# Two heads' attention scores in the row halves of TensorE's array, with the gate sums added by VectorE

## The chip, the cores and the metric

The kernel runs on one core of one Trainium2 chip. The metric is the device time of one execution in microseconds. The engines are TensorE (PE in the profile, its weight loads PEld), VectorE (DVE), ScalarE (ACT), GpSimd (POOL) and SyncE (SP), which here only issues transfers.

## What is computed

Four post-norm layers over 256 positions of width 1024. Layers 0 and 3 mix tokens by forgetting attention ("fox": 16 heads of 64, causal, with a bias from cumulated log forget gates), layer 1 by an S5 state-space mixer, layer 2 by pooling. Each mixer is followed by a norm, a SwiGLU FFN and a norm. What matters here:

```python
log_f = jax.nn.log_sigmoid((x @ w_f + b_f))
c = jnp.cumsum(log_f, axis=1)                       # per position and head
logits = einsum('bqhd,bkhd->bhqk', qb, k) * scale   # scale = 1/8
logits = logits + cb[..., :, None] - c_k[..., None, :]
logits = jnp.where(mask, logits, -inf)              # causal
p = softmax(logits)                                 # then p @ v, @ w_o
```

The term of the query, cb, is the same along a row and drops out of the softmax; the kernel adds only the key's term, kept as eight times the negated sum, so that the scale of the exponential (0.125) serves both.

## The kernel before

Weights stream as tiles of 128 x 1024 f32 (512 KB). SyncE loads a tile into one of four raw buffers once VectorE is done with the tile four earlier; ScalarE rounds it to a high half (L617, semaphore w_hi), VectorE subtracts for the low half (L1021, w_lo), and TensorE forms three products of every pair of operands in place of one (L1628 to L1630, 256 columns; L1637 to L1643, 512 columns). `w_used` counts the tiles that TensorE is done with, and frees their places. Each engine's order is the order in which the code for that engine is written; engines meet only in semaphores.

A fox layer has tiles 0 to 7 for V, then for each of eight pairs of heads p one tile for Q and one for K, then tiles 24 to 31 for the output projection. The loop step j of TensorE does the products of Q and K of pair j (banks 4 and 5), turns the probabilities of pair j-2 (L1931, `probs_turned`), forms the scores of pair j-1 (L1948 and L1949) and the output products of pair j-2 (L1960, L1961; head s writes to PSUM partitions 64s to 64s+63, so each head has a half of the array's columns). Pair 7's scores and the last two pairs' probabilities follow among the first output projections (`out_half`).

Queries and keys are copied head by head from PSUM to buffers of 80 partitions (L783 by ScalarE, L1283 by VectorE): 64 of the head, and 16 rows below in which the keys' buffer holds the gate sums of all heads (L754) and the queries' buffer a one for the head's own row (L747 in layer 0 by ScalarE, L566 in layer 3 by GpSimd). The score product so adds the gate sums itself. VectorE then adds the causal mask and takes the row maxima (L1255 for the first 128 queries, L1257 for the others, `masked`), ScalarE takes the exponentials (L800, L802), VectorE scales (`scaled`, L1244 to L1246).

GpSimd computes parameters of the S5 layer in `s5_parameters` (L486 to L532) during the first attention: a flag `zz_ready` (L525) lets VectorE scale the B matrices (`s5_scale`, L1372, from j = 5 on). Then it fills a piece of slot[2] with zeros and stores it eight times to `toep` in HBM (L573), and loads the rows of the norm (L584). The matrices B and C of the S5 layer come through SyncE's queue (L453) into slot[1] and slot[3]; ScalarE changes C's signs at L812 and L816, at the end of the fox layer.

Behind the last output projection VectorE forms the residual sum and statistics of the norm (L1037, L1041, `ln`); TensorE turns the normed activations next (L1608).

## Time and profile before

| | |
|---|---|
| median of 3 runs | 1169.89 us (1168.87 to 1171.18) |
| the profiled execution | 1169.65 us |
| its span, first to last instruction | 1167.9 us |
| busy: TensorE, weight loads, VectorE, ScalarE, GpSimd | 1150.9, 1068.3, 819.2, 601.4, 161.3 us |
| mean granted clock of TensorE | 0.999 of full speed |
| moved by DMA | 221.14 MB, mean 189 GB/s |

The span leaves out what lies around the instructions, so the time is 1.75 us above it. Matmuls are pipelined: the start of one to the start of the next tells how long it holds TensorE, its own duration is longer. A row "x6" is several instructions merged, with the time from the first's start to the last's end. In rows of a window, the busy times of the engines stand in order, each with its number of instructions.

### The profile page before, as it was taken

To read this page: it belongs to the slowest core of one execution; us is meant where nothing else is said; L and a number is where in the kernel's file an instruction comes from. 1 tells how busy PE (TensorE), PEld (TensorE's weight loads), DVE (VectorE), ACT (ScalarE), POOL (GpSimd) and SP (SyncE) were. 2 spreads that over 40 slices of the span, in tenths; PEclk is the share of its full clock that TensorE was granted. 3 is DMA by queue.
4 is the path that set the end of the run, shared out by engine and by line. 5 is a ranking of instruction groups with operands and counts; after the bars stand their busy time and mean duration, and the time that the engine had idled before them with its cause. 6 is when DMAs were issued, how large, how long until landed. Compare 5 with 4: busy or idle time off the path is not lost.

```text
span 1167.9 us, 22245 instructions
## 1 busy us (share of the span) xinstructions
PE 1150.9 (99%) x9166; PEld 1068.3 (91%) x9166; DVE 819.2 (70%) x1263; ACT 601.4 (51%) x947; POOL 161.3 (14%) x212
## 2 busy tenths in 40 slices
PE   8999999999999999999999999999999999999997
PEld 7998899999977779999998899999989988999996
DVE  7789899989868687455466776554587768654545
ACT  6777544544445456354444555444438664644441
POOL 0650099002970000000000000000010000000000
PEclk9999999999999999999999999999999999999999
DMA  6676454554756558565654556656536334856540
GB/s 243 219 269 228 160 198 151 193 181 175 235 167 211 181 180 300 178 226 180 202 170 162 198 180 236 201 180 205 190 101 241 130 109 146 277 188 200 182 163 37
DMA packets 63981, 221.14 MB, mean 189 GB/s; under 512 B 8068, under 2 KB 9988, under 8 KB 63368
## 3 DMA queue, kind: packets, MB, share of 16 engines
q1 hardware_dynamic: 57224, 202.57, 50.8%
q0 software_dynamic: 5648, 15.73, 4.1%
q8 instruction: 73, 1.20, 0.4%
q10 hardware_dynamic: 1008, 1.41, 0.4%
q14 instruction: 28, 0.23, 0.1%
HBM read 211.03 MB, written 7.60 MB: 187 GB/s over the span
## 4 chain that ended last, share of the span: by engine, by line
PE 93%; DVE 4%; DMA 1%; ACT 1%; issue 1%; SPq 0%; DVEq 0%; ACTq 0%
PE bank L1660 18%; PE bank L1628 15%; PE bank L1629 15%; PE bank L1630 15%; PE bank L1758 5%; PE bank L1692 4%; PE bank L1637 3%; PE bank L1643 3%; PE bank L1639 3%; DMA raw<-in_w 1%; PE bank L1949 1%; PE bank L1608 1%; PE bank L1793 1%; PE bank L1931 1%; PE bank L1960 1%; PE bank L1948 1%
## 5 line engine op out<-in xcount | busy, mean ns | idle before, releaser
L1021 DVE TENSOR_TENSOR wlo<-raw,whi 128x1024 fp32r<-128x1024 f32 x227 | 288.3, 1277 | 61.2 <-ACT whi L617 60.3
L617 ACT ACTIVATE whi<-raw 128x1024 fp32r<-128x1024 f32 x227 | 239.0, 1056 | 76.5 <-PE bank L1660 29.1
L1628 PE MATMUL bank<-xboth,whi 128*128 128x256 f32 x936 | 261.3, 279 | 0.0
L1629 PE MATMUL bank<-xboth,whi 128*128 128x256 f32 x936 | 259.3, 277 | 0.0
L1630 PE MATMUL bank<-xboth,wlo 128*128 128x256 f32 x936 | 259.2, 277 | 0.0
L1021 DVE TENSOR_TENSOR ext<-raw,ext 128x1024 fp32r<-128x1024 f32 x142 | 172.3, 1222 | 42.3 <-ACT ext L617 42.1
L1628 PEld LDWEIGHTS bank<-xboth,whi 128*128 128x128 f32 x936 | 176.2, 188 | 1.1 <-issue 0.9
L1629 PEld LDWEIGHTS bank<-xboth,whi 128*128 128x128 f32 x936 | 175.9, 188 | 0.1
L1630 PEld LDWEIGHTS bank<-xboth,wlo 128*128 128x128 f32 x936 | 175.8, 188 | 0.0
L617 ACT ACTIVATE ext<-raw 128x1024 fp32r<-128x1024 f32 x142 | 148.9, 1056 | 45.8 <-PE bank L1660 22.5
L1628 PE MATMUL bank<-xboth,ext 128*128 128x256 f32 x600 | 167.2, 279 | 0.0
L1629 PE MATMUL bank<-xboth,ext 128*128 128x256 f32 x600 | 166.0, 277 | 0.0
L1630 PE MATMUL bank<-xboth,ext 128*128 128x256 f32 x600 | 166.0, 277 | 0.0
L1169 DVE TENSOR_TENSOR hval<-bank,silu 128x256 f32<-128x256 f32 x80 | 33.8, 423 | 159.8 <-PE bank L1630 159.7
L1628 PEld LDWEIGHTS bank<-xboth,ext 128*128 128x128 f32 x600 | 112.8, 188 | 0.9 <-issue 0.9
L1629 PEld LDWEIGHTS bank<-xboth,ext 128*128 128x128 f32 x600 | 112.8, 188 | 0.1
L1630 PEld LDWEIGHTS bank<-xboth,ext 128*128 128x128 f32 x600 | 112.7, 188 | 0.0
L703 ACT ACTIVATE hhi<-hval 128x256 fp32r<-128x256 f32 x72 | 30.0, 417 | 127.5 <-DVE hval L1169 125.4
L698 ACT ACTIVATE silu<-bank 128x256 f32<-128x256 f32 x80 | 30.5, 381 | 99.3 <-PE bank L1630 99.3
L584 POOL DMA_DIRECT2D slot<-in_ln_row x16 | 8.6, 545 | 446.0 <-DVE x_tm L1093 395.7
L1660 PE MATMUL bank<-ext,hhi 128*128 128x256 f32 x448 | 61.8, 281 | 0.0
L1660 PE MATMUL bank<-whi,hlo 128*128 128x256 f32 x376 | 59.6, 281 | 0.0
(383 smaller groups left out, 2036.1 us busy)
## 6 DMA issues: line engine op xcount, KB each, us to landing
raw<-in_w SPq DMA_DIRECT2D x370, 512.0 KB, 4.3
slot<-in_ln_row POOLq DMA_DIRECT2D x16, 512.0 KB, 5.1
toep<-slot POOLq DMA_DIRECT2D x8, 512.0 KB, 8.5
toepA<-toep SPq DMA_DIRECT2D x2, 1024.0 KB, 6.5
BT<-toep SPq DMA_DIRECT2D x2, 1024.0 KB, 7.3
x_tm<-in_x SPq DMA_DIRECT2D x2, 512.0 KB, 5.2
slot<-in_s_B SPq DMA_DIRECT2D x2, 512.0 KB, 5.6
slot<-in_s_C SPq DMA_DIRECT2D x2, 512.0 KB, 5.8
```

Of the source, the lines that this page charges most:

```text
L617: nc.scalar.activation(hi_of(c), raw[:, c % RAW, :], ACT.Copy).then_inc(w_hi, 1)
L1021: V.tensor_tensor(lo_of(c), raw[:, c % RAW, :], hi_of(c).bitcast(F32), ALU.subtract).then_inc(w_lo, 1)
L1169: V.tensor_tensor(hval[:, :], bank[5][:, 0:SEQ], silu[:, :], ALU.mult).then_inc(h_ready, 1)
L1628: mm(dst, wh, bhi[:, kc, :], start=(i == 0), stop=False)
L1629: mm(dst, wh, blo[:, kc, :], start=False, stop=False)
L1630: ins = mm(dst, wl, bhi[:, kc, :], start=False, stop=(i == len(chunks) - 1))
L1637: mm(banks[2 * m + j][:, :], a_hi[:, cols], hi_of(c)[:, j * HALF:(j + 1) * HALF], start=first, stop=False)
L1639: mm(banks[2 * m + j][:, :], a_hi[:, cols], lo_of(c)[:, j * HALF:(j + 1) * HALF], start=False, stop=False)
L1643: ins = mm(banks[2 * m + j][:, :], a_lo[:, cols], hi_of(c)[:, j * HALF:(j + 1) * HALF], start=False, stop=last)
L1660: ins = mm(banks[2 * m + q // 2][:, q % 2 * SEQ:(q % 2 + 1) * SEQ], a[:, cols], w[:, q * SEQ:(q + 1) * SEQ], start=start and q % 2 == 0, s ...
L1692: return mm(banks[b][:, :], (a_lo if lo_act else a_hi)[:, cols], (lo_of if lo_w else hi_of)(c)[:, half], start=False, stop=stop)
L1758: return mm(out, x[:, kc, m * P:(m + 1) * P], w[:, 0:4, kc * P:(kc + 1) * P], start=start, stop=stop)
```

## The change

- **Scores.** Queries and keys of a pair lie in 128 partitions, head 0 in 0 to 63 and head 1 in 64 to 127, one copy for both. The scores of a head are a product over 64 rows of the array; the order is now both heads' 128-column products, then both heads' 256-column products.
- **Gate sums.** VectorE adds a tile `decay` in place of the constant mask: gate sums of the keys, the same in all partitions, with the mask in it. GpSimd makes it: it stores the gate sums to HBM (`gates_out`), loads them spread to 128 partitions pair by pair (`decay_load`, 256 KB), and adds the mask (`decay_causal`, two additions of 256 columns a pair). `masked` waits for it. In layer 0 eight such stops are put ahead of and into `s5_parameters`; in layer 3 they are a loop by itself, in which each load waits for a query copy.
- **Zeros.** The stores of zeros start before the gate sums, and go on one a stop.
- **C.** C's loads move behind the attention (its buffer slot[3] now holds masked sums), ahead of the weight tiles F0 + 2 = 34 and F0 + 3 = 35; its sign changes move to chunks 3 and 4 of the first FFN.
- The rows of ones and the copies of gate sums below keys and queries go.

```diff
@@ SyncE
+                if c in (F0 + 2, F0 + 3):
+                    part = slice((c - F0 - 2) * D, (c - F0 - 1) * D)
+                    sp.wait_ge(s_sb, HEADS)
+                    sp.dma_start(slot[3][:, part], t["s5_C"][:, part]).then_inc(c_landed, 16)
@@ GpSimd
+            def gates_out(f):
+                pool.wait_ge(gate_c, f + 1)
+                pool.dma_start(gates, zg[:, 0, :]).then_inc(gates_stored, 16)
+                pool.wait_ge(gates_stored, 16 * (f + 1))
+            def decay_load(f, p):
+                heads = slice(2 * p, 2 * p + 2)
+                pool.dma_start(decay_of(f)[:, heads, :, :].rearrange("p h j k -> p (h j k)"),
+                               gates[heads, :].rearrange("h k -> (h k)").partition_broadcast(P)).then_inc(decay_landed[p % 2], 16)
+            def decay_causal(f, p):
+                decay, corner = decay_of(f), corner_of(f)
+                tri = cst[:, C_MASK:C_MASK + P].unsqueeze(1).to_broadcast([P, 2, P])
+                heads = slice(2 * p, 2 * p + 2)
+                pool.wait_ge(decay_landed[p % 2], 16 * (PAIRS // 2 * f + p // 2 + 1))
+                TT(corner[:, heads, :], decay[:, heads, 0, :], tri, ALU.add).then_inc(decay_masked, 1)
+                TT(decay[:, heads, 1, :], decay[:, heads, 1, :], tri, ALU.add).then_inc(decay_masked, 1)
...
-                        s5_parameters()
                         step(nc.gpsimd.memset(slot[2][:, 0:D], 0.0))
-                        for k in range(8):
-                            pool.dma_start(t["toep"][:, k * D:(k + 1) * D], slot[2][:, 0:D]).then_inc(zero_st, 16)
+                        pool.wait_ge(gate_z, 1)
+                        zeros_out(0)
+                        zeros_out(1)
+                    gates_out(f)
+                    decay_load(f, 0)
+                    decay_load(f, 1)
+                    if s5_next:
+                        pair = [0]
+                        def pause():
+                            p = pair[0]
+                            decay_causal(0, p)
+                            if p + 2 < PAIRS:
+                                decay_load(0, p + 2)
+                                zeros_out(p + 2)
+                            pair[0] += 1
+                        for p in range(3):
+                            pause()
+                        s5_parameters(pause)
                         pool.wait_ge(zero_st, 16 * 8)
+                    else:
+                        for p in range(PAIRS):
+                            decay_causal(f, p)
+                            if p + 2 < PAIRS:
+                                pool.wait_ge(q_sb, PAIRS * f + p + 1)
+                                decay_load(f, p + 2)
@@ ScalarE
-                        for s in range(2):
-                            nc.scalar.copy(qa_of(f)[0:HD, 2 * j + s, :], bank[4][s * HD:(s + 1) * HD, 0:SEQ]).then_inc(q_sb, 1)
+                        nc.scalar.copy(qa[:, j, :], bank[4][:, 0:SEQ]).then_inc(q_sb, 1)
@@ VectorE
-                        V.tensor_tensor_reduce(logits[:, s, 0:P], bank[6 + s][:, 0:P], cst[:, C_MASK + P:C_MASK + 2 * P], 1.0, NEG,
+                        h = 2 * p + s
+                        dve.wait_ge(decay_masked, HEADS * f + 2 * p + 2)
+                        V.tensor_tensor_reduce(logits[:, s, 0:P], bank[6 + s][:, 0:P], corner_of(f)[:, h, :], 1.0, NEG,
                                                ALU.add, ALU.max, smx[:, s, 0:1])
-                    for s in range(2):
-                        V.tensor_copy(ka[0:HD, 2 * j + s, :], bank[5][s * HD:(s + 1) * HD, 0:SEQ]).then_inc(k_sb, 1)
+                    V.tensor_copy(ka[:, j, :], bank[5][:, 0:SEQ]).then_inc(k_sb, 1)
@@ TensorE
+                    pe.wait_ge(q_sb, E1 + p + 1)
+                    pe.wait_ge(k_sb, E1 + p + 1)
+                    if p >= 1:
+                        pe.wait_ge(s_sb, E2 + 2 * p)
+                    rows = [slice(s * HD, (s + 1) * HD) for s in range(2)]
                     for s in range(2):
-                        h = 2 * p + s
-                        if p >= 1:
-                            pe.wait_ge(s_sb, E2 + 2 * (p - 1) + s + 1)
-                        mm(bank[6 + s][:, 0:P], qa_of(f)[:, h, 0:P], ka[:, h, 0:P], start=True, stop=True)
-                        mm(bank[6 + s][:, P:3 * P], qa_of(f)[:, h, P:SEQ], ka[:, h, :], start=True, stop=True).then_inc(s_ps, 1)
+                        mm(bank[6 + s][:, 0:P], qa[rows[s], p, 0:P], ka[rows[s], p, 0:P], start=True, stop=True)
+                    for s in range(2):
+                        mm(bank[6 + s][:, P:3 * P], qa[rows[s], p, P:SEQ], ka[rows[s], p, :], start=True, stop=True).then_inc(s_ps, 1)
```

TensorE, the middle of loop step 2 of the first fox layer (scores of pair 1), before:

```order
L1931 MATMUL bank1<-cst,sc 128x128 x2
L1948 MATMUL bank6<-ka,qa_first 128x128 [waits s_sb,k_sb,q_sb]
L1949 MATMUL bank6<-ka,qa_first 128x256
L1948 MATMUL bank7<-ka,qa_first 128x128 [waits s_sb]
L1949 MATMUL bank7<-ka,qa_first 128x256
L1960 MATMUL bank2<-pT,vt 64x256 [waits pT_sb]
L1961 MATMUL bank2<-pT,vt 64x128
```

and now, in the same place:

```order
L1972 MATMUL bank1<-cst,sc 128x128 x2
L1983 MATMUL bank6<-ka,qa 128x128 [waits s_sb,k_sb,q_sb]
L1983 MATMUL bank7<-ka,qa 128x128
L1985 MATMUL bank6<-ka,qa 128x256
L1985 MATMUL bank7<-ka,qa 128x256
L1996 MATMUL bank2<-pT,vt 64x256 [waits pT_sb]
L1997 MATMUL bank2<-pT,vt 64x128
```

The four products alternate between the heads' banks, and only the first has waits.

GpSimd, from its first work in the program, now (before, the row of the first `lam` product, L505, was its first work; lines L512 and L493 are the old L505 and L486):

```order
L600 MEMSET slot 128x1024 [waits cst_landed]
L591 DMA toep<-slot 128x1024 [waits gate_z,pool_own]
L591 DMA toep<-slot 128x1024
L571 DMA gates<-zg 16x256 [waits gate_c]
L577 DMA decay_first<-gates 128x512 [waits gates_stored]
L577 DMA decay_first<-gates 128x512
...
L586 TENSOR_TENSOR slot<-decay_first,cst 128x256 [waits decay_landed0]
L587 TENSOR_TENSOR decay_first<-decay_first,cst 128x2x128
L577 DMA decay_first<-gates 128x512
L591 DMA toep<-slot 128x1024
...
L512 TENSOR_TENSOR lam<-slot 128x64 [waits mag_ready,prm_act,prm_landed]
```

Three stops of four instructions stand ahead of the parameters now; three more follow inside them before `zz_ready`, and two behind it.

SyncE, the loads of C, before (two loads of C, ahead of the weight tiles 17 and 19):

```order
L453 DMA slot<-in_s_C 128x1024 [waits w_lo]
L460 DMA raw<-in_w 128x1024
L460 DMA raw<-in_w 128x1024 [waits w_lo]
L453 DMA slot<-in_s_C 128x1024 [waits w_lo]
L460 DMA raw<-in_w 128x1024
```

and now (ahead of the weight tiles 34 and 35):

```order
L467 DMA raw<-in_w 128x1024 [waits w_lo] x18
L460 DMA slot<-in_s_C 128x1024 [waits s_sb,w_lo]
L467 DMA raw<-in_w 128x1024
L460 DMA slot<-in_s_C 128x1024 [waits s_sb,w_lo]
L467 DMA raw<-in_w 128x1024
```

Two weight tiles in a row each have a load of C in front of them on the queue.

## Rows read from the trace of the kernel before

**Rows 1.** The page: busy time, share of the span, instructions.
```profile
PE 1150.9 (99%) x9166; PEld 1068.3 (91%) x9166; DVE 819.2 (70%) x1263; ACT 601.4 (51%) x947; POOL 161.3 (14%) x212
```
**Rows 2.** Busy time by stretch, 20 to 25 us.
```profile
core 0: us, PE busy (x) PEld busy (x) DVE busy (x) ACT busy (x) POOL busy (x), PEclk, DMA share, GB/s
20.00:25.00 5.00, 5.00 (x24) 4.10 (x23) 4.46 (x12) 4.93 (x6) 0.00 (x0) 1.00 0.30 107
```
**Rows 3.** Timeline of TensorE, scores and output products of one step.
```profile
53.95 0.39 PE L1948 MATMUL bank<-ka,qa_first 80*128 80x128 f32 x2
...
54.61 0.38 PE L1948 MATMUL bank<-ka,qa_first 80*128 80x128 f32 x2
...
55.35 0.66 PE L1960 MATMUL bank<-pT,vt 128*64 128x256 f32 x4
55.84 0.40 PE L1961 MATMUL bank<-pT,vt 128*64 128x128 f32 x4
56.16 0.38 PE L1628 MATMUL bank<-xboth,whi 128*128 128x256 f32 x1
```
**Rows 4.** The same, two windows of 0.04 and 0.06 us within the output products.
```profile
55.35 0.44 PE L1960 MATMUL bank<-pT,vt 128*64 128x256 f32 x2
...
55.62 0.39 PE L1960 MATMUL bank<-pT,vt 128*64 128x256 f32 x2
```
**Rows 5.** Timeline of TensorE, transposes of 32 rows in the S5 layer.
```profile
351.13 1.95 PE L2033 MATMUL bank<-cst,slot 32*128 32x32 f32 x32
...
372.47 0.69 PE L2095 MATMUL bank<-cst,slot 32*128 32x32 f32 x32 [0.72 <-ACT slot L854]
```
**Rows 6.** Timeline of VectorE in the first fox layer.
```profile
24.75 0.68 DVE L1229 TENSOR_TENSOR_SCAN zg<-ones,zg 16x256 f32<-16x256 f32 x1
...
48.12 0.29 DVE L1255 CUSTOM_DVE_ANT_0 sc<-bank,cst 128x128 f32<-128x128 f32 x1
...
79.32 0.87 DVE L1283 COPY ka<-bank 64x256 f32<-64x256 f32 x2
...
83.21 1.23 DVE L1372 TENSOR_TENSOR slot<-slot 128x1024 f32<-128x1024 f32 x1
```
**Rows 7.** SyncE's weight loads (512 KB each) issued from 105.8 to 119.9 us.
```profile
DMA to landing us min/median/max: 3.4/3.9/4.7
```
**Rows 8.** Timeline of GpSimd in the first fox layer.
```profile
37.15 0.32 POOL L505 TENSOR_TENSOR lam<-slot 128x64 f32<-128x64 f32 x1 [36.71 <-ACT slot L758]
...
46.82 1.84 POOL L486 TENSOR_TENSOR slot<-lam 128x256 f32<-128x256 f32 x1
...
52.11 0.86 POOL L491 TENSOR_TENSOR lam<-slot 128x256 f32<-128x256 f32 x1
...
59.19 0.10 POOL L525 MEMSET slot<- 128x1 f32 x1
...
91.18 1.08 POOL L584 DMA_DIRECT2D slot<-in_ln_row  x2 [13.69 <-DMA toep<-slot]
```
**Rows 9.** Busy time by stretch, single steps of the attention loops.
```profile
79.45:87.89 8.44, 8.44 (x72) 7.76 (x71) 7.91 (x23) 6.00 (x16) 0.00 (x0) 1.00 1.02 401
87.89:96.39 8.50, 8.50 (x72) 7.95 (x71) 8.03 (x24) 6.20 (x17) 1.08 (x2) 1.00 0.92 355
...
928.40:936.80 8.40, 8.40 (x72) 7.72 (x71) 6.32 (x22) 5.53 (x15) 0.00 (x0) 1.00 0.38 126
```
**Rows 10.** Waits in 98 to 140 us: total, times, longest.
```profile
PEld bank L1931 <- DVE sc_last L1246: 0.8, 2, 0.4
```
**Rows 11.** Timelines of SyncE, ScalarE, VectorE, end of the first attention.
```profile
111.62 0.33 SPq L460 DMA_DIRECT2D raw<-in_w  x1
...
116.77 1.06 ACT L617 ACTIVATE whi<-raw 128x1024 fp32r<-128x1024 f32 x1 [0.30 <-PE bank L1643]
...
116.38 3.49 DVE L1021 TENSOR_TENSOR wlo<-raw,whi 128x1024 fp32r<-128x1024 f32 x3
120.21 0.69 DVE L1037 SCALAR_TENSOR_TENSOR x_tm<-x_tm,bank 128x512 f32<-128x512 f32 x1 [0.34 <-PE bank L1692]
```
**Rows 12.** Timeline of ScalarE in the first FFN.
```profile
162.16 0.38 ACT L698 ACTIVATE silu<-bank 128x256 f32<-128x256 f32 x1 [1.62 <-PE bank L1630]
```

More of the change, by code:

```diff
@@ L64 @@
 C_MASK = C_PERM + P
-C_HOT = C_MASK + 2 * P
-C_SGN = C_HOT + HEADS
+C_SGN = C_MASK + P
 C_NSGN = C_SGN + 1
@@ L169, in build @@
         turn = sb("turn", [P, GROUPS])
-        sb("to_512", [P, 4])
+        sb("to_512", [P, 148])
         raw = sb("raw", [P, RAW, D])
@@ L231, in build, with decay_of, corner_of @@
         ext_hi, ext_lo = ext[:, :, 0, :], ext[:, :, 1, :]
-        def qa_of(f):
-            return (qa_first, qa_late)[f]
+        def decay_of(f):
+            return (decay_first, decay_late)[f]
+        def corner_of(f):
+            return slot[(3, 1)[f]][:, :].rearrange("p (h k) -> p h k", h=HEADS)
         h_tm = [slot[0][:, m * SEQ:(m + 1) * SEQ] for m in range(TM)]
@@ L378, in build @@
         LATER = {0: [(dcol[:, :], t["s5_dcol"]), (pscale[:, :], t["pool_scale"])]}
-        for i, (where, name) in enumerate(((1, "s5_B"), (1, "s5_B"), (3, "s5_C"), (3, "s5_C"))):
-            part = slice(i % 2 * D, (i % 2 + 1) * D)
-            LATER[2 * i + 1] = [(slot[where][:, part], t[name][:, part])]
+        for i in range(2):
+            part = slice(i * D, (i + 1) * D)
+            LATER[2 * i + 1] = [(slot[1][:, part], t["s5_B"][:, part])]
         N_LATER = sum(len(v) for v in LATER.values())
@@ L561, in _ @@
                 if kind == "fox":
[L564 to L574 removed]
+                    f = l // 3
+                    s5_next = l == 0 and layers > 1
+                    if s5_next:
+                        step(nc.gpsimd.memset(slot[2][:, 0:D], 0.0))
+                        pool.wait_ge(gate_z, 1)
[4 more added lines that the diff above has]
+                    decay_load(f, 1)
+                    if s5_next:
+                        pair = [0]
[7 more added lines that the diff above has]
+                        for p in range(3):
+                            pause()
+                        s5_parameters(pause)
+                        pool.wait_ge(zero_st, 16 * 8)
+                    else:
[4 more added lines that the diff above has]
+                                decay_load(f, p + 2)
                 for k in range(2):
@@ L726, in ffn @@
                     chunk(c)
+                    if s5_here and c in (3, 4):
+                        act.wait_ge(c_landed, 32)
+                        half = slot[3][:, (c - 3) * D:(c - 2) * D]
+                        nc.scalar.activation(half, half, ACT.Copy, scale=nsgn if c == 3 else -1.0).then_inc(c_signed, 1)
                     if s5_here and 5 <= c < 13:
@@ L744, in fox @@
                         nc.scalar.activation(zg[:, 2, :], zg[:, 2, :], ACT.Ln, bias=1.0).then_inc(gate_l, 1)
-                    if l == 0 and c in (3, 4, 6, 7):
-                        i = (3, 4, 6, 7).index(c)
-                        ins = nc.scalar.copy(qa_of(0)[HD:KQ, 4 * i:4 * i + 4, :],
-                                             cst[HD:KQ, C_HOT + 4 * i:C_HOT + 4 * i + 4].unsqueeze(2).to_broadcast([HEADS, 4, SEQ]))
-                        if i == 3:
-                            ins.then_inc(qa0_rows, 1)
-                    if c == 5:
-                        act.wait_ge(gate_c, f + 1)
-                        nc.scalar.copy(ka[HD:KQ, :, :], zg[:, 0, :].unsqueeze(1).to_broadcast([HEADS, HEADS, SEQ])).then_inc(ka_rows, 1)
                 if l == 0 and layers > 1:
@@ L808, in fox @@
                         hi_to(T1 + KC - 2)
-                if l == 0 and layers > 1:
-                    act.wait_ge(later_landed, 16 * N_LATER)
-                    nc.scalar.activation(slot[3][:, 0:D], slot[3][:, 0:D], ACT.Copy, scale=nsgn).then_inc(c_signed, 1)
                 for c in range(KC - 1):
                     hi_to(min(T0 + KC + 2 * PAIRS + c + 2 + ahead_at(l, PAIRS + c), T0 + T_FOX + AHEAD - 1))
-                if l == 0 and layers > 1:
-                    nc.scalar.activation(slot[3][:, D:2 * D], slot[3][:, D:2 * D], ACT.Copy, scale=-1.0).then_inc(c_signed, 1)
             def s5(l, n):
```

50 lines of the change are left out of this document (20 added, 30 removed).

## The prediction

> **What bounds the kernel now.** The page comes first [rows 1]: TensorE is busy for 99% of the span, VectorE for 70%, GpSimd for 14%. So a microsecond counts only if it is taken out of TensorE's own stream or makes TensorE wait. Second, the stretch ahead of the attention [rows 2]: in 20 to 25 us TensorE is busy for 5.00 of 5.00 us, with DMA at a share of 0.30. The copies that ScalarE makes there are covered, and so is their removal.
>
> Third, TensorE's timeline of one head pair [rows 3]. Every matmul of f32 operands leaves two records, here called passes. One head's scores run from 53.95 to 54.61, 0.66 us: two passes of 128 columns (0.11 each) and two of 256 (0.22 each). The second head costs the same, so scores hold TensorE for 1.31 us a pair, to 55.27. The output products that follow (L1960, L1961) have the same columns, but each head has its own half of the array's columns, and all eight passes lie between 55.35 and about 56.06. Narrower windows show why [rows 4]: two records of L1960 stand in the window that ends at 55.40, before either head's second pass, which start together at 55.62. In program order the second head's first pass is the fifth record. So halves of the array run side by side, and the second does not wait for the first's remaining passes. What such a group costs around itself can be read off too: 0.09 us between the scores' end and 55.35, and a first pass that holds 0.27 instead of 0.22, together 0.14 to enter; behind it 0.10 to the next matmul at 56.16, and as much again for that one's held first pass (an estimate by the entering pass and its length of 0.38), so 0.20 to leave.
>
> **The change on TensorE.** Scores of both heads become 64-row products in two row halves, into banks 6 and 7. Before, 80 rows were used, which admits no second product. The trace has no 64-row product. The nearest rows are transposes of 32 rows [rows 5]: 32 records of L2033, which stay mostly in one row group, take 1.95 us, and 32 records of L2095, which go round all four, take 0.69. Row groups do overlap, then, though for short products. I price the pair like the outputs: 0.65 (two passes of 0.11, two of 0.22) + 0.14 to enter = 0.79 against 1.31, a saving of 0.52. Six of the eight pairs of a layer (pairs 1 to 6) are followed by outputs in column halves, which paid for entering before as well: 12 x 0.52 = 6.2 us over both fox layers. Pairs 0 and 7 are followed by products over the full array, so leaving is new: 0.52 - 0.20 = 0.32, four times 1.3. Gross gain 7.5 us. Bounds: entering free gives 9.7 gained; no overlap at all costs 16 x 0.14 + 4 x 0.20 = 3.0, a loss.
>
> The Trainium skill speaks against part of this: "TensorEngine Tiling (Array Packing)", Key Properties, says that a change of tiling mode drains the engine; this trace agrees, with its 0.09 and 0.10 us gaps. "TensorE: Matmul & The Clock Gate", Part 3, gives 3.07 times for four row tiles, an efficiency of 0.77; by that two tiles would be worth 1.54, a pair 0.85 instead of 0.79, and the gross gain about 6.5 us.
>
> **Copies.** Q's and K's copies go from two of 64 partitions to one of 128 with as many columns. VectorE's two take 0.87 us together [rows 6], so it saves 0.43 a pair. The head indicator and gate rows on ScalarE (before the attention) and GpSimd vanish; TensorE is busy over them anyway: nothing.
>
> **GpSimd's new work, first layer.** The gate sums end at 24.75 + 0.68 = 25.4 us, pair 0's mask is used at 48.12 [rows 6]. A store and a load of, say, 3.4 to 4.7 us each (what 512 KB takes, [rows 7]) put pair 0 in SBUF at about 33. One stop for a pair is two additions of 256 columns and two DMA issues. Six operations of that width run from 46.82 to 52.97, 1.03 each with gaps, and two issues take 1.08 [rows 8], so 3.1 us a stop. Pair 0 is ready near 35, 12 us early; later pairs are needed every 7.9 us. The work queued behind the stops matters more: VectorE's scaling at 83.21 [rows 6] waits for the flag that GpSimd sets at 59.19. That work takes 59.19 - 37.15 = 22.0 us [rows 8], six stops now lie ahead of it: 33.3 + 6 x 3.1 + 22.0 = 74, and the scaling comes at 83.21 - 2.4 = 80.8 (0.32 and four times 0.52 earlier). Cost nothing, 6.6 us to spare; it fails from 4.2 us a stop. At the slowest such addition, 1.84 us [rows 8], a stop is 4.8 and the flag 3.3 us late. The layer norm rows that GpSimd loads after this move from 91.18 [rows 8] to about 95 and are used only after the norm's sums of 120.21 [rows 11]: nothing. The early zero stores meet a DMA share of 0.30 [rows 2], so nothing. In the last layer VectorE is busy for 6.32 of 8.40 us [rows 9] and each load has two pairs' time: nothing.
>
> **VectorE at the end of the first attention.** It is busy for 7.91 of 8.44 us and for 8.03 of 8.50 [rows 9]. TensorE already waits for its last probabilities, 0.8 us over the two heads [rows 10]. From pair 5's K copy to there TensorE loses 3 x 0.52 + 0.32 = 1.9 us of work and VectorE 3 x 0.43 = 1.3. The wait grows by 0.6; GpSimd, until now finished by 79.45, still works beside it, for which I add 0.4. Together 1.0 us, between 0 and 3. In the last layer, with its slack, 0.
>
> **The loads of C.** They leave their places in the middle of the attention on SyncE's queue and now stand ahead of the weight tiles 34 and 35. SyncE waits there for the last mask, which VectorE has done before the split of tile 30 that the queue waits for anyway: nothing. But tile 35 is issued at 111.62 [rows 11] and lands at most 4.7 us later, 116.3 [rows 7], and ScalarE rounds it from 116.77. Two more 512 KB ahead of it at the densest rate seen, 401 GB/s [rows 9], are 2.6 us: landed 118.9, rounded 120.0, and VectorE's third split, which began at 118.7, ends 1.3 us late. The next thing on VectorE is the layer norm's first residual sum at 120.21, which had waited 0.34 for TensorE. Its statistics release TensorE's transposes, with no filler left: about 1.0 us. Bounds 0, and 6 if the C loads and the tiles never overlap (3.9 us each). ScalarE's two sign passes, 1024 columns each like the rounding of a tile (1.06 us), move out of this place into the FFN, where ScalarE waits 1.6 us for TensorE at each silu [rows 12]: nothing.
>
> **Sum.** The profiled execution took 1169.65 us (span 1167.9), 0.24 under the median. 1169.65 - 7.5 + 1.0 + 1.0 = 1164.2, as a median 1164.4.
>
> **The rivals.**
> - *Row halves start strictly in program order.* The second head's first pass would wait for the first head's second. The eight passes in the new order would start at 0, 0.11, 0.11, 0.22, 0.22, 0.44, 0.44 and 0.66 and end at 0.88 instead of 0.65: saving 0.29 for twelve pairs and 0.09 for four, 3.9 gross, less 1.0 for C and 0.5 for the growing wait: 1167.3, as a median 1167.5. The output products' rows speak against it [rows 4], but those are column halves, and the transposes of [rows 5] stand in round order, which fits both. "TensorE: Matmul & The Clock Gate", Part 3 of the Trainium skill, states this order for matmuls; the output products here disagree. Chance 13%.
> - *VectorE or GpSimd takes it in the first attention.* Stops near 4.8 us, or VectorE slowed beside GpSimd in its fullest stretch: another 2 to 3.3 us lost, about 1167. For it: 94% busy; against: 6.6 us to spare. 15%.
> - *The change doesn't do what it says, slower.* Two 64-row products run one behind the other and each group only pays for entering and leaving: 1169.65 + 3.0 + 1.0 = 1173.7, median 1174. It decides once a pair's scores take over 1.31 - 0.14 = 1.17 us. Against it stand [rows 5]. 7%.
> - *As forecast*: 63%, its own range 1161.8 to 1166.5. 2% for the rest.
>
> **The numbers.** The range takes the free entering and C loads at the low end to some extent, 1161.3, and the first two rivals and a costly C load at the high end, 1169.3. Under 0.2% (2.3 us) a measurement can hardly tell from no change, so faster means below 1167.6. Nearly all of the forecast and two thirds of the first two rivals: 80%. Within: 11%. Slower: 9%.
>
> **What the profile of after would show.** Right: the score groups span about 0.8 us a pair, with two records of the 128-column product at the same start; tiles 34 and 35 rounded some 2 us later relative to TensorE; a longer wait at the last probabilities. Wrong: 128-column starts 0.11 apart; VectorE waiting for GpSimd at a mask or at the first scaling; TensorE idle for over 1 us at the first norm's transposes.

## The result, and the profile after

The kernel after took 1172.51 us (median of 15 runs, 1170.61 to 1173.85), the kernel before beside it 1170.41 us (15 runs). The ratio is 1.0018, 95% interval 1.001 to 1.0026: some 2 us slower, where 6 us faster was forecast. The profiled execution took 1171.09 us (span 1169.1); against the one of before, 1.4 us more. It lies 1.4 us under its median, the one of before 0.8.

The page, busy times (answers to [rows 1]); TensorE has the same matmuls, GpSimd 35 us more work:

```profile
PE 1150.3 (98%) x9166; PEld 1062.0 (91%) x9166; DVE 820.3 (70%) x1247; ACT 583.5 (50%) x925; POOL 196.2 (17%) x261
```

TensorE's timeline of one step, scores and output products (answers to [rows 3]):

```profile
51.93 0.60 PE L1972 MATMUL bank<-cst,sc 128*128 128x128 f32 x4
52.46 0.49 PE L1983 MATMUL bank<-ka,qa 64*128 64x128 f32 x4
52.78 0.60 PE L1985 MATMUL bank<-ka,qa 64*128 64x256 f32 x4
53.78 0.81 PE L1996 MATMUL bank<-pT,vt 128*64 128x256 f32 x3 [0.40 <-ACT pT L839]
```

The eight passes (two records per product and head) start two by two: at 52.458 and 52.465, 52.672 and 52.678 those of 128 columns, at 52.783 and 52.790, 53.002 and 53.008 those of 256. The two heads run side by side, and from the first start to the next group it is 0.86 us wherever nothing else waits (here ScalarE's copies add to it). The scores do nearly what they were priced at. What went wrong lies around them.

VectorE and, under it, GpSimd in one step of the last layer (L1061 is the subtraction for the low half, called split pass or split below):

```profile
911.25 2.90 DVE L1061 TENSOR_TENSOR ext<-raw,ext 128x1024 fp32r<-128x1024 f32 x1
914.08 0.41 DVE L1324 COPY ka<-bank 128x256 f32<-128x256 f32 x1
914.41 1.21 DVE L1061 TENSOR_TENSOR ext<-raw,ext 128x1024 fp32r<-128x1024 f32 x1
```

```profile
911.08 0.54 POOL L577 DMA_DIRECT2D decay_late<-gates  x1 [3.84 <-ACT qa L829]
911.63 0.74 POOL L586 TENSOR_TENSOR slot<-decay_late,cst 128x256 f32<-128x256 f32 x1
912.33 0.73 POOL L587 TENSOR_TENSOR decay_late<-decay_late,cst 128x256 f32<-128x256 f32 x1
```

The same split pass takes 1.21 us alone and 2.90 beside GpSimd's two additions, which last 1.43 and are not slowed: the split ends 1.1 us behind the second, as if it had only then begun. The same happens at 893.82, 920.23 and 929.18. From 911 us on each of these loads waits for ScalarE's query copy, and so the additions behind it fall on the step's first split.

Who gives way follows who comes first. In the four cases GpSimd's issue of the load stands 0.17 to 0.42 us ahead of the split. In e4 (below), where the steps are longer, the split comes 0.15 us ahead of the issue, passes in 1.22 us, and the addition takes 1.10 in place of 0.74:

```profile
912.23 1.22 DVE L1061 TENSOR_TENSOR ext<-raw,ext 128x1024 fp32r<-128x1024 f32 x1
```

```profile
912.38 0.54 POOL L577 DMA_DIRECT2D decay_late<-gates  x1 [4.52 <-ACT qa L829]
912.94 1.10 POOL L586 TENSOR_TENSOR slot<-decay_late,cst 128x256 f32<-128x256 f32 x1
```

It is so again at 920.86 and 929.48 of e4. Why an issue that stands first makes the split wait for both additions, no run shows; alone it does not (e2, below).

TensorE's weight loads, what they waited for (total, times, longest), 895 to 970 us:

```profile
PEld bank L1972 <- DVE sc L1286: 2.5, 6, 1.0
...
PEld bank L1972 <- DVE sc_last L1286: 0.8, 2, 0.4
```

and 46 to 104 us, first of after, then of before:

```profile
PEld bank L1972 <- DVE sc L1286: 2.7, 7, 1.0
...
PEld bank L1996 <- ACT pT L839: 1.1, 2, 0.8
```

```profile
PEld bank L1960 <- ACT pT L793: 0.3, 1, 0.3
PEld bank L1931 <- DVE sc L1246: 0.2, 1, 0.2
```

TensorE now waits for probabilities (tile sc) in the steps of both attentions, 2.7 and 2.5 us, where before it did so for 0.2 us in the first and not at all in the last. Only the 0.8 us for the last pair (sc_last) were there before.

At the first norm (answers to [rows 11]; SyncE, then ScalarE and VectorE, then TensorE):

```profile
109.20 0.33 SPq L460 DMA_DIRECT2D slot<-in_s_C  x1
109.57 0.43 SPq L467 DMA_DIRECT2D raw<-in_w  x1
110.33 0.33 SPq L460 DMA_DIRECT2D slot<-in_s_C  x1
...
118.58 1.06 ACT L670 ACTIVATE whi<-raw 128x1024 fp32r<-128x1024 f32 x1 [1.44 <-DMA raw<-in_w]
...
119.68 1.23 DVE L1061 TENSOR_TENSOR wlo<-raw,whi 128x1024 fp32r<-128x1024 f32 x1 [1.28 <-ACT whi L670]
120.82 0.68 DVE L1077 SCALAR_TENSOR_TENSOR x_tm<-x_tm,bank 128x512 f32<-128x512 f32 x1
...
123.82 0.39 PE L1733 MATMUL bank<-ext,olo 128*128 128x512 f32 x1
125.49 0.66 PE L1649 MATMUL bank<-cst,x_tm 128*128 128x128 f32 x4 [1.28 <-DVE x_tm L1133]
```

From the last filler to the transposes are 1.67 us; before, 0.39 (125.12 to 125.51).

Windows of before and of after in the S5 layer, the last columns the granted clock, DMA share and GB/s:

```profile
365.00:366.00 1.00, 1.00 (x47) 1.00 (x40) 0.91 (x4) 0.15 (x1) 0.00 (x0) 1.00 0.51 213
```

```profile
363.00:364.00 1.00, 0.41 (x4) 0.30 (x3) 0.94 (x3) 0.79 (x3) 0.00 (x0) 1.00 0.61 254
...
365.00:366.00 1.00, 1.00 (x24) 1.00 (x20) 0.91 (x4) 0.09 (x1) 0.00 (x0) 0.50 0.00 0
```

For 3.4 us from 364.9 the chip granted TensorE 1.2 GHz in place of 2.4. From 363 to 364 TensorE had been busy for 0.41 us; it was so before too, without the fall.

All kernels have the same 9166 matmul records, so the start of one record can be compared across profiles. The table gives how much each stretch is longer than in the profile of before; the columns end at 30, 103 (end of the first attention), 126 (first norm), 355, 372 (the S5 stretch above), 890, 1000 (last attention) and 1159 us of before.

```
                      start  att.1   norm  ..355  ..372  ..890  att.4  ..end     sum
after                  -1.1   -0.3   +1.4   +0.1   +1.6   +0.7   -1.2   +0.0    +1.3
e1_c_later             +0.7   -0.3   +0.2   +0.2   +0.0   -0.3   -0.8   +0.1    -0.3
e2_no_adds             -0.9   -1.2   +0.9   +0.2   +1.6   -0.1   -3.7   -0.0    -3.3
e3_halves_alone        +0.1   -3.4   -0.1   +0.1   -0.0   -0.5   -3.9   +0.0    -7.6
e4_one_half            +0.1   +1.5   +1.4   +0.1   +0.0   -0.4   +1.7   +0.0    +4.5
e5_zeros_late          -0.9   -0.6   +4.1   +0.8   +0.0   +0.3   -0.8   +0.0    +2.9
e6_late_unheld         +0.0   +0.1   +2.3   +0.1   +0.0   +1.1   -3.0   +0.0    +0.5
e7_before_c            +0.2   +0.1   +2.0   +0.0   +0.0   -0.1   +0.2   +0.4    +2.8
e8_head_order          +0.4   -0.4   +1.6   +0.1   +1.6   +0.4   -1.2   +0.0    +2.6
e9_c_unheld            +0.1   -0.3   +0.1   -0.0   +0.0   -0.1   -3.1   +0.0    -3.3
e10_halves_zeros       -0.7   -4.0   -0.1   -0.0   +1.6   +0.2   -3.9   +0.0    -6.9
e11_c_vector_adds      +0.0   -0.8   +0.1   +0.2   +1.6   -0.0   -0.1   +0.0    +1.0
e12_zeros_mid          -1.1   -0.5   +0.2   +0.2   +1.6   +0.4   -0.1   +0.0    +0.7
e13_no_adds_first      -0.0   -3.7   -0.0   -0.0   +0.0   +1.5   -2.0   +0.0    -4.2
e14_vector_early       +0.2   +4.8   -0.1   +0.1   +0.0   +0.8   -3.3   +0.0    +2.5
```

The start column is when the first tiles happened to land. Neither it nor the half-speed stretch at 365 us, which is worth +1.6 where it is there, follows an edit. Each row is a single execution: from 372 to 890 us all the kernels have the same code, and the column there runs from -0.5 to +1.5. So a difference of 1 us in a long stretch says little by itself. The +4.8 of e14 has a half-speed stretch of its own in it (below).

### The profile page after: what moved, and what is told of

Same layout as the page of the kernel before. It is cut to its first block, busy times and chain, and to the rows that moved or that the text cites. A ratio compares the mean times of both kernels' runs of the same rounds, so it can differ in the third digit from the quotient of the medians.

```text
span 1169.1 us, 22268 instructions
## 1 busy us (share of the span) xinstructions
PE 1150.3 (98%) x9166; PEld 1062.0 (91%) x9166; DVE 820.3 (70%) x1247; ACT 583.5 (50%) x925; POOL 196.2 (17%) x261
## 4 chain that ended last, share of the span: by engine, by line
PE 84%; DVE 9%; ACT 3%; issue 2%; DMA 2%; SPq 0%; ACTq 0%; DVEq 0%
PE bank L1701 18%; PE bank L1669 13%; PE bank L1671 13%; PE bank L1670 13%; PE bank L1799 5%; PE bank L1733 4%; PE bank L1678 3%; PE bank L1680 3%; PE bank L1684 3%; DMA raw<-in_w 2%; DVE wlo L1061 1%; PE bank L1649 1%; PE bank L1834 1%; DVE ext L1061 1%; ACT sc L848 1%
## 5 line engine op out<-in xcount | busy, mean ns | idle before, releaser
L1061 DVE TENSOR_TENSOR wlo<-raw,whi 128x1024 fp32r<-128x1024 f32 x227 | 290.0, 1283 | 63.1 <-ACT whi L670 62.1
L1061 DVE TENSOR_TENSOR ext<-raw,ext 128x1024 fp32r<-128x1024 f32 x142 | 178.3, 1264 | 40.0 <-ACT ext L670 39.7
```

The source lines that it names most:

```text
L1061: V.tensor_tensor(lo_of(c), raw[:, c % RAW, :], hi_of(c).bitcast(F32), ALU.subtract).then_inc(w_lo, 1)
```

## The experiments

Times are medians, ratios against before on the same chip with 95% intervals. The theory at the start: halves gain as priced; lost again to C's loads, to VectorE held beside GpSimd, and to crowded transfers at 42 to 54 us. Rivals: row halves gain nothing; one of the three losses alone is the whole of it.

**e3, row halves and single copies on the kernel before.** The gate sums are left out of the scores altogether; no GpSimd additions, no spread loads, C as before.

```diff
-                        mm(bank[6 + s][:, 0:P], qa_of(f)[:, h, 0:P], ka[:, h, 0:P], start=True, stop=True)
+                        mm(bank[6 + s][:, 0:P], qa[rows[s], p, 0:P], ka[rows[s], p, 0:P], start=True, stop=True)
...
```

> Edit on the kernel before: queries and keys of two heads in 128 partitions and the scores in row halves, nothing else; the gate sums are left out of the scores, with ScalarE's 3.6 us copy of them, so no GpSimd additions, no new loads, and C and the zeros where they were. Theory 1 (the halves gain, the rest of the change takes it back): 5.5 to 7 us faster than before. Rival (VectorE and ScalarE bound the attention loop, so shorter scores only turn into waits): at most 2 us faster.

1162.0 us, ratio 0.9929 (0.9917 to 0.9941), more than the 5.5 to 7 us expected. The two attentions gain 3.4 and 3.9 us, near the 7.5 priced for the halves. By the spacing of the groups alone it is 6.6 (0.46 us for each of twelve pairs, 0.26 to 0.31 for the four others); where the other 0.7 comes from is not separated (the edit also makes one copy of two and drops ScalarE's copy of the gate sums).

**e4, both heads in one row half** (head 1's scores are then head 0's).

```diff
-                    rows = [slice(s * HD, (s + 1) * HD) for s in range(2)]
+                    rows = [slice(0, HD) for s in range(2)]
```

> Edit: both heads' scores are computed from head 0's 64 rows, so from one row half; same instructions and waits otherwise, the second head's scores are wrong. Theory 1 (halves run side by side): the four products take 1.3 us instead of 0.76, TensorE holds 0.55 us longer per pair, 8.8 us over 16 pairs less what is now hidden of its waits, so 4 to 8 us slower than the changed kernel. Rival (the waits are what bounds the loop, the halves gain nothing): within 1.5 us of the changed kernel.

1175.29 us, ratio 1.0044 (1.003 to 1.0058).

```profile
54.53 0.71 PE L1983 MATMUL bank<-ka,qa 64*128 64x128 f32 x4
55.08 1.03 PE L1985 MATMUL bank<-ka,qa 64*128 64x256 f32 x4
56.04 0.44 PE L1996 MATMUL bank<-pT,vt 128*64 128x256 f32 x2
```

A group takes 1.5 us (54.53 to 56.04) and not 0.86, in all sixteen pairs: 0.65 more each, 10.4 in all. Yet the kernel is only 2.8 us above after (4 to 8 were expected). In after, waits for probabilities fill that time; here only the last pair waits for them, and in the last attention the additions hold no split for more than 0.4 us.

**e8, the score products head by head.**

```diff
                     for s in range(2):
                         mm(bank[6 + s][:, 0:P], ...)
-                    for s in range(2):
                         mm(bank[6 + s][:, P:3 * P], ...)
```

> The kernel after with the four score products in the old order: head 0's 128 and 256 columns, then head 1's. Theory (the two row halves run side by side whatever the order, as records 7 ns apart suggest and as the output products do): the scores take the same 0.65 us a pair, and the time is within 0.5 us of the kernel after. Rival (products start strictly in program order): head 1's first pass waits until head 0's second pass of 128 columns and first of 256 have started, the group takes about 0.88 us or more instead of 0.65, and both fox layers lose up to 3.7 us, less what waits for VectorE hide: a median of 1173.5 to 1176.

1171.95 us, ratio 1.0007 (0.9993 to 1.002), the attentions as in after.

```profile
53.94 0.50 PE L1983 MATMUL bank<-ka,qa 64*128 64x128 f32 x4
54.26 0.61 PE L1984 MATMUL bank<-ka,qa 64*128 64x256 f32 x4
54.80 0.82 PE L1995 MATMUL bank<-pT,vt 128*64 128x256 f32 x4
```

The group takes the same 0.86 us. The four passes of L1983, two of each head, all start before the first of L1984, and head 1's first starts 13 ns after head 0's (53.952 and 53.939), though three more of head 0's passes stand ahead of it in the program. "TensorE: Matmul & The Clock Gate", Part 3 of the Trainium skill, has matmuls start strictly in program order; this trace disagrees.

**e7, C's loads and sign changes moved, on the kernel before.**

```diff
+                if c in (F0 + 2, F0 + 3):
+                    part = slice((c - F0 - 2) * D, (c - F0 - 1) * D)
+                    sp.dma_start(slot[3][:, part], t["s5_C"][:, part]).then_inc(c_landed, 16)
...
```

> The kernel before with one part of the change alone: the two loads of C stand ahead of tiles 34 and 35 and its sign changes in chunks 3 and 4 of the first FFN. Theory (the loads make tiles 34 and 35 late and with them the first norm): the gap of TensorE ahead of the first norm's transposes grows from 0.4 to 1.2 to 1.7 us, a loss of about 1 us, a median of 1171 to 1171.5 where before has 1170.4. Rival (the stall comes from the shorter attention of the changed kernel, in which VectorE arrives at the norm with less lead): the gap stays below 0.6 us and the time is that of before within 0.3 us.

1172.54 us, ratio 1.0007 (0.9996 to 1.0018). The medians differ by 1.9 us, though the interval of the ratio takes in no change; the loss is read at the first norm, 2.0 us:

```profile
122.09 1.23 DVE L1023 TENSOR_TENSOR wlo<-raw,whi 128x1024 fp32r<-128x1024 f32 x1 [1.31 <-ACT whi L621]
...
125.40 0.39 PE L1694 MATMUL bank<-ext,olo 128*128 128x512 f32 x1
127.90 0.66 PE L1610 MATMUL bank<-cst,x_tm 128*128 128x128 f32 x4 [2.12 <-DVE x_tm L1095]
```

**e1, after with C ahead of tiles 40 and 41.**

```diff
-                if c in (F0 + 2, F0 + 3):
+                if c in (F0 + 8, F0 + 9):
...
```

> Edit: the two loads of C go six weight tiles later (ahead of tiles 40 and 41), their sign passes two chunks later. Theory 1, the C loads cost the first norm 1.3 to 1.5 us, because tile 35 lands late: VectorE reaches the first residual sum in time again, the gap of TensorE before the first norm's transposes (1.67 us from start to start in the changed kernel) returns to 0.4, the kernel gains 1.3 us. Rival: the stall is what TensorE's earlier arrival leaves of a VectorE chain that did not get shorter, then the gap stays above 1.4 us and nothing is gained.

1169.67 us, ratio 0.999 (0.9981 to 1.0), 2.8 us under after. The norm costs 0.2 us in place of 1.4, the transposes again follow 0.39 us behind the last filler (125.68 to 126.07). e1 and e7 together settle C: 1.2 to 2.0 us. Of the rest of the 2.8, about 1 us goes with the clock (its mean over the runs is 0.9977 in e1 and 0.9967 in after).

**e2, no additions on GpSimd** (one-element memsets in their place; the causal mask is left out).

```diff
-                TT(corner[:, heads, :], decay[:, heads, 0, :], tri, ALU.add).then_inc(decay_masked, 1)
+                nc.gpsimd.memset(corner[:, 2 * p, 0:1], 0.0).then_inc(decay_masked, 1)
...
```

> Edit: GpSimd's sixteen pairs of mask additions become single-element writes, loads and waits stay; the causal mask is left out of the scores. Theory 1, VectorE is held while GpSimd adds (its 1.22 us passes take 2.7 to 2.9 us at five places of the last layer, 7.2 us in all): these passes fall to 1.22 us, TensorE's waits for probabilities in the last layer (3.3 us) nearly vanish, and the kernel gains 2 to 4 us. Rival, TensorE waits because the scores no longer cover ScalarE's copies of the turned probabilities: VectorE's passes get shorter but the kernel gains under 1 us.

1168.57 us, ratio 0.9984 (0.9973 to 0.9994). The last attention gains 3.7 us, every split there is back at 1.22 (one at 909.08 begins 0.17 us behind the issue of a load, as in after), and no wait for a pair's probabilities but the last is left. The first gains only 1.2, for a new reason. Shorter stops issue loads and stores sooner; one weight tile takes 12.57 us, in the chain of waits that leads to 60 us:

```profile
41.72 12.57 DMA raw<-in_w
...
54.32 1.07 ACT whi L670
```

**e5, zeros stored behind the S5 parameters**, as before.

```diff
-                                zeros_out(p + 2)
...
+                        for k in range(8):
+                            zeros_out(k)
```

> The kernel after, but all eight stores of zeros stand behind the S5 parameters on GpSimd, as before the change; the stops keep only the spread gate sums. Theory (the early stores crowd the weight loads): between 42 and 54 us the DMA share falls from above 1.0 to about 0.8, ScalarE's waits for raw buffers there shrink from 5.9 us to 2 or less, output products of step 2 no longer wait some 0.7 us for ScalarE's copies, and the first attention ends 1 to 2 us earlier against the kernel after: a median near 1171. Rival 1 (VectorE held beside GpSimd's additions is all that matters there): nothing moves by more than 0.5 us. Rival 2 (the stores are only shifted): they now start near 95 us, run beside the loads of C and tiles 34 and 35, and the stall ahead of the first norm's transposes grows from 1.7 to 3 us or more, so the median is 1172 to 1174.

1177.05 us, ratio 1.005 (1.0035 to 1.0065). The first attention moves by 0.3 us: as long as GpSimd adds, the zeros' crowding is not what it lost. The second rival holds, at a higher price: the stores run into the loads of C, and TensorE stands idle for 3.65 us. The profiled execution, 1172.63 us, is among the shortest of the twelve.

```profile
123.71 0.39 PE L1731 MATMUL bank<-ext,olo 128*128 128x512 f32 x1
127.75 1.11 PE L1647 MATMUL bank<-cst,x_tm 128*128 128x128 f32 x4 [3.65 <-DVE x_tm L1131]
128.52 1.20 PE L1731 MATMUL bank<-ext,ohi 128*128 128x512 f32 x2
```

In that gap the clock fell to 1.2 GHz (for 3.4 us from 127.05): two passes behind it take 1.20 where after has 0.71.

**e6, the last layer's loads not held by query copies.**

```diff
-                                pool.wait_ge(q_sb, PAIRS * f + p + 1)
```

> The kernel after, but in the last layer the loads of the spread gate sums no longer wait for query copies, so that GpSimd makes its sixteen additions one behind another at the start of the last attention. Theory (VectorE is held while GpSimd adds, and it costs where VectorE is late for the probabilities): VectorE's split passes are still stretched from 1.2 to up to 2.9 us, but all in the stretch from the gate sums on, where TensorE does not wait for probabilities; the TensorE waits for probabilities of 895 to 965 us (2.5 us) fall below 1, and the last attention gains about 2 us more: median near 1170.5. Rival (the missing 2.5 us of the last layer have another cause, such as the DMA of the spread gate sums or the alternating score order): the waits stay, and the time is within 0.5 us of the kernel after, 1172 to 1173.

1169.61 us, ratio 0.9988 (0.9976 to 1.0), 2.9 under after; the last attention gains 3.0 in place of 1.2. The additions do not all fall before the attention as I had written, but at 893 to 917 us; they hold fewer splits (the worst takes 1.75 us), and the wait for probabilities shrinks (895 to 970 us; after: 2.5):

```profile
PEld bank L1971 <- DVE sc L1285: 0.5, 1, 0.5
```

**e10, e3 with the zero stores early.** Gate sums again left out.

> The kernel before with row halves and single copies (gate sums left out), as an earlier run, which gained 3.3 us over the first attention; and in addition the eight stores of zeros early: two before the first attention and six inside GpSimd's parameters, from about 34 to 64 us. No spread gate sums are loaded. Theory (the early stores crowd the weight loads): the DMA share at 42 to 54 us is above 0.95, ScalarE waits for raw buffers, and 1 to 2 us of the 3.3 are lost there: a median of 1163 to 1164. Rival (only stores and spread loads together crowd it, or VectorE's holds are all): the first attention keeps its gain within 0.5 us, a median of 1162 or, since GpSimd's stores no longer run at 69 to 100 us, a little less.

1162.71 us, ratio 0.9935 (0.9923 to 0.9948). The share at 42 to 54 us is 0.95, at 343 GB/s, and the first attention gains 4.0 us, no less than e3. So the zeros alone, without spread loads, take nothing.

**e13, e6 and e1's edits, the first layer's additions left out** (with them part of the causal mask there; the spread loads stay, zeros at the stops of pairs 3 to 6).

> The kernel with C later and the last layer's loads not held, and in the first layer GpSimd's additions replaced by one-element memsets (that layer's 128-query maxima then lack the mask of their block, and so do its other products). The spread gate sums are still loaded; the stores of zeros stand at the stops of pairs 3 to 6, two each. Theory A (VectorE held beside GpSimd's additions costs the first attention its gain): TensorE no longer waits 4.8 us for probabilities between 46 and 104 us but under 1, and that attention gains 3 us or more against before instead of 0.4: a median of 1164.5 to 1165.5. Theory B (the spread loads and what they crowd out cost it): the gain stays at 0.4 to 1.2 us, a median of 1166.5 to 1168.

1165.5 us, ratio 0.9949 (0.9936 to 0.9962). The first attention gains 3.7 us with all spread loads in place. TensorE's waits for probabilities, 46 to 104 us, here and then in e9, whose only other difference is where the zeros are stored:

```profile
PEld bank L1972 <- DVE sc_last L1286: 0.4, 1, 0.4
PEld bank L1972 <- DVE sc L1286: 0.3, 1, 0.3
```

```profile
PEld bank L1971 <- DVE sc L1285: 3.5, 7, 1.0
```

With the additions the zeros' place hardly matters (-0.3 in after, -0.5 in e12 below, -0.6 in e5). With the zeros at the later stops and the additions gone, the gain is back: the additions are worth 3.1 to 3.4 us there. But the additions alone are not the whole account: e2, without them and with the zeros as in after, has -1.2. Behind the one limit stands the other, the crowded transfers, worth 2.5 us, and only both edits together give the gain back.

Nor is it the additions' own time alone. In after GpSimd's S5 parameters end at 93.1 us (before: 71.8; e13: 77.8), pushed back by the stops, and they hold VectorE too, or are held. By an estimate from the medians of each form, VectorE's instructions from 44 to 104 us are 4.9 us longer in after, 1.8 before and 1.0 in e13; about half of the 4.9 lies beside parameters. The last attention of e13 shows 2.0 us of gain where e9 with the same code there has 3.1: which splits the additions meet, and who comes first, may be the cause, but no run separates it.

**e9, e1 and e6 together.**

> The kernel after with two edits at once: C's loads ahead of tiles 40 and 41, and the last layer's loads of spread gate sums not held back by query copies. Alone they were worth 2.8 and 2.9 us at the medians. Theory (two separate losses in two separate places): both gains stand, less what of the medians' difference is the clock, 3.9 to 5.7 us together, a median of 1167 to 1168.6, below the kernel before (1170.5). Rival (they share a cause, or one is noise of the clock): at most 3 us, a median above 1169.4.

1167.73 us, ratio 0.9984 (0.9974 to 0.9994): 4.8 under after, 2.4 under before. Most of the two gains adds up (4.8 of 5.7), and this complete kernel beats both.

**e11, e1 and VectorE adding the mask in the last layer, ahead of the maxima.**

```diff
...
+                    if f == 1:
+                        tri = cst[:, C_MASK:C_MASK + P].unsqueeze(1).to_broadcast([P, 2, P])
+                        heads = slice(2 * p, 2 * p + 2)
+                        dve.wait_ge(decay_landed[p % 2], 16 * (PAIRS // 2 * f + p // 2 + 1))
+                        V.tensor_tensor(corner_of(f)[:, heads, :], decay_of(f)[:, heads, 0, :], tri, ALU.add).then_inc(decay_masked, 1)
+                        V.tensor_tensor(decay_of(f)[:, heads, 1, :], decay_of(f)[:, heads, 1, :], tri, ALU.add).then_inc(decay_masked, 1)
                     for s in range(2):
                         dve.wait_ge(s_ps, E2 + 2 * p + s + 1)
```

> The kernel after with C's loads ahead of tiles 40 and 41, and in the last layer VectorE itself adds the mask to the spread gate sums, two additions of 256 columns a pair ahead of the maxima; GpSimd there only loads. Theory (the loss is that VectorE is held while GpSimd adds, and VectorE has 2 us of slack a step in the last layer): VectorE's split passes there take 1.22 us each, and the last attention gains 3.3 to 3.8 us against before instead of 1.2: a median of 1166.5 to 1168, at or below the one with the loads not held. Rival (16 more operations of 0.3 to 0.7 us ahead of the maxima delay the scores' exponentials and so the probabilities): the last attention gains under 2 us, a median above 1169.

1170.86 us, ratio 1.0001 (0.9993 to 1.001): the rival (VectorE's additions come ahead of the maxima and delay the exponentials). From 890 to 950 us TensorE gains 2.2 us on before, and by 960 it has given it all back, at the last two pairs, whose additions stand on the path from the scores to the exponentials:

```profile
952.35 0.35 DVE L1284 TENSOR_SCALAR sc<-sc,smx 128x256 f32<-128x256 f32 x1
952.61 0.42 DVE L1293 TENSOR_TENSOR slot<-decay_late,cst 128x256 f32<-128x256 f32 x1
952.94 0.42 DVE L1294 TENSOR_TENSOR decay_late<-decay_late,cst 128x256 f32<-128x256 f32 x1
953.51 0.29 DVE L1301 CUSTOM_DVE_ANT_0 sc_last<-bank,slot 128x128 f32<-128x128 f32 x1
```

**e12, e11 with zeros at the stops of pairs 3 to 6.**

> As the one with C later and VectorE adding the mask in the last layer, and with no zero store before the first attention: two stores each at the stops of pairs 3 to 6, from about 45 to 68 us. Theory (stores, spread loads and weight tiles crowd the stretch from 36 to 54 us): the share there falls, ScalarE's waits for raw buffers shrink, and the first attention gains 0.5 to 1.5 us. Rival (it only moves the crowding some 8 us on, where B's loads follow): within 0.5 us of that kernel.

1169.77 us, ratio 1.0001 (0.9992 to 1.001); in the first attention -0.5 against e11's -0.8: nothing, though the share at 42 to 54 us falls to 0.87.

**e14, e1 and VectorE adding in both layers, at the ends of steps 0 to 4.**

> C later, and no addition on GpSimd in either layer: VectorE adds the mask to the spread gate sums at the ends of loop steps 0 to 4 (pairs 0 and 1, 2, 3 and 4, 5 and 6, 7), up to two pairs, 1.5 us, a step, well ahead of the maxima. Theory A (VectorE has room in steps 0 to 4 and only holds and late maxima cost): no stretched split pass but those beside GpSimd's S5 parameters; the first attention gains 2 us or more, the last 3.5: a median of 1163 to 1166, the fastest kernel of all. Theory B (VectorE's room in the steps is already spent, or the first layer's loss lies in the transfers): the first attention gains under 1 us, a median of 1166.5 to 1169.

1171.79 us, ratio 1.0005 (0.9992 to 1.0018), slower than either theory had it. The last attention gains 3.3 us, as theory A has it; the first loses 4.8. One weight tile comes late, as in e2 (ScalarE's waits, 46 to 104 us), and VectorE, with 1.7 us more in a step, does not catch up:

```profile
ACT whi L668 <- DMA raw<-in_w: 5.5, 2, 4.7
```

VectorE's lateness then empties TensorE (busy for 0.08 us from 74 to 75), and for 3.4 us from 76.8 the clock falls to 1.2 GHz:

```profile
75.65 0.55 PE L1980 MATMUL bank<-cst,sc 128*128 128x128 f32 x3 [1.57 <-DVE sc L1284]
```

```profile
77.00:78.00 1.00, 1.00 (x7) 0.93 (x8) 1.00 (x3) 0.48 (x1) 0.92 (x2) 0.50 0.00 0
```

Up to 1.7 of the 4.8 us (half of the 3.4, an estimate) are the clock's. So crowding does cost, where GpSimd's stops are short enough to issue the transfers close together. This kernel with its zeros later was not run, so whether VectorE's additions would pay in the first attention is open.

## Why the prediction was wrong

- **Scores: right, the saving a little smaller than priced.** A pair's scores to the next group took 1.40 us [rows 3] and take 0.86; entering costs 0.20 us behind the last turn, before 0.11. Together 0.46 saved against 0.52 priced, 6.6 us in all against 7.5. e3's two attentions gain 7.3, of which the groups explain 6.6. Program order (13%) and no overlap (7%) are refuted by the starts in pairs, by e8 and by e4.
- **"In the last layer VectorE is busy for 6.32 of 8.40 us ... nothing": the step that failed.** I counted GpSimd's time and VectorE's slack, and not that one holds the other. A pair's two additions (1.43 us) add up to 1.7 us to the split pass they meet when GpSimd comes first, and TensorE waits 2.5 us for probabilities; e2 and e6 put the loss at 1.8 to 2.5 us.
- **The first attention, "I add 0.4. Together 1.0 us".** Same failure, larger: e13 against e9 and e12 puts it at 3.1 to 3.4 us. The rival *VectorE or GpSimd takes it* had the mechanism and (2 to 3.3 us) the price, with 15%. Its first condition was not needed, and its place was half right: by the starts of the score groups after loses 0.8 us against e3 in each of the two steps from 52.5 to 70.1 us, where VectorE was busy for about 7.0 of 8.5 us before, and 1.3 from 70 us on. The flag came at 75.07 (forecast 74), the scaling at 82.23 (80.8) without waiting for it. That the flag fits is in part luck: the first three stops took 12.0 us and not 9.3, with 3.24 of waiting for a spread load to land that was in no term, and the work behind them took 29.2 and not 31.3. The 6.6 us to spare held, and were not what mattered.
- **C's loads, 1.0 us: mis-sized.** Right chain (the tile was rounded at 119.6, forecast 120.0); the norm lost 1.4 us in after, 2.0 in e7. With 1.28 us of idle TensorE at the transposes, the prediction's own sign of being wrong had come.
- **Early zeros, "DMA share of 0.30, so nothing".** By luck half right. The 0.30 is of 20 to 25 us, and most zeros go out later: from 42 to 54 us the share is 1.06 instead of 0.71, and the three weight tiles issued there take 11.0 us to land at the median instead of 7.3. In after this cost hardly more than the 0.40 us for which TensorE waits at 53.78 for ScalarE's copies; it is worth 2.5 us once the additions are gone (e2 against e13).
- **The clock: not in the sum.** The mean over the runs is 0.9967 in after and 0.9977 in the 101 runs of before beside the experiments; 0.001 of 1170 us is 1.2 us, an estimate. The profile's stretch of 3.4 us cost 1.6. Why it appears in the profiles of after, e2, e8, e10, e11 and e12 and not in the other ten stays open.

By the profile: in place of -7.5 the halves gave -7.3 (e3), and in place of +1.0 and +1.0 after has +3.1 and +2.7 in the attentions (its columns against e3's), +1.4 (C), +1.6 (clock), -1.1 (first landing). With +0.7 between 372 and 890 us, which no experiment explains, and +0.1, that is +1.2, where the profiles differ by +1.3.

## What to carry to other kernels

Work moved to an idle engine is priced by what it does to the engine beside it: here two GpSimd additions stopped a VectorE pass until both were done, unless the pass had begun first. So they belong where VectorE has slack *and* nobody soon waits for it. Tying them to an event of every step can place them on the same instruction each time, and 0.2 us then decide who waits. The same additions on VectorE itself cost less time (0.42 us each) but are on the path if they stand between scores and exponentials. And a load moved on a queue is paid where the tiles behind it are consumed: six tiles further on, C's cost almost nothing (0.2 us). Removing one limit may bring out the next: in the first attention the additions hid the crowded transfers.

## What the runs showed of the hardware

- VectorE's 128x1024 subtraction: 1.22 us alone, 2.67 to 2.90 beside two GpSimd additions of 0.7 us each whose load GpSimd began to issue 0.17 to 0.42 us before it. Where the subtraction begins first it keeps its 1.22, and the addition takes 1.10 (e4, 912.94) or 1.78 (after, 932.35) in place of 0.74.
- The issue of a load alone holds nothing: in e2, which has the loads and no additions, GpSimd's issue begins at 908.91 and the split at 909.08, and it takes 1.22 us.
- Products in different row halves start 7 to 14 ns apart, and a later product does not wait for earlier ones of the other half.
- A 512 KB tile took 12.57 us to land while the DMA share was 1.03.
- TensorE's clock fell to 1.2 GHz for 3.4 us in an idle stretch of 3.65 us (e5), at 76.8 us of e14, where TensorE had been busy for 0.43 us from 74 to 76, and near 365 us in six profiles and not in the other ten (the microsecond with 0.41 us of work stands in after and before alike).
